# Four raw and three split weight slots, and modulation sums on an earlier, tighter schedule, in a two-block transformer kernel

## The reference, cut to what matters

```python
def hybrid_layer(x, c, positions, w_mod, b_mod, g_pre, g_post, w_in, w_out, ...):
    mod = jax.nn.silu(c) @ w_mod + b_mod          # 2048 x 6144 a layer
    shift, scale, gate = jnp.split(mod, 3, axis=-1)
    h = rms_norm(x, g_pre) * (1.0 + scale[:, None, :]) + shift[:, None, :]
    proj = h @ w_in
    ...
    out = y @ w_out
    return x + gate[:, None, :] * rms_norm(out, g_post)
```

## Time and profile before

| | |
|---|---|
| three runs | 3748.43, 3752.31, 3753.46 us; median 3752.31 |
| profiled execution | 3751.18 us, span 3749.5 us, mean granted TensorE clock 0.981 |
| TensorE busy | 3533.7 us, 94% |
| VectorE, ScalarE, GpSimd busy | 1865.1, 1322.7, 1155.9 us |
| DMA | 494.65 MB, mean 132 GB/s |
| chain that ended last | TensorE 66%, DMA 13%, VectorE 12%, ScalarE 6% |

### The profile page before, as it was taken

The page is one execution under the profiler, slowest core; times in us unless marked ns, Lnnn a source line. Parts: engine busy times, 40 slices in busy tenths (PEclk is TensorE's granted clock), DMA queues, the critical chain, the costliest instruction groups (busy, mean ns, idle before and its releaser), DMA issues.

```text
span 3749.5 us, 47967 instructions
## 1 busy us (share of the span) xinstructions
PE 3533.7 (94%) x17180; PEld 2823.6 (75%) x17180; DVE 1865.1 (50%) x3156; ACT 1322.7 (35%) x2206; POOL 1155.9 (31%) x1244
## 2 busy tenths in 40 slices
PE   6799999999879999999998999999998999999997
PEld 5667878887666678788876778877886778877885
DVE  4643376553565233765435535545535534645535
ACT  4212323332442223233325525423235525423223
POOL 5554766664362546666610000002000000002000
PEclk9999999999989999999999999999999999999999
DMA  8544454455674445544645632322345632322345
GB/s 274 150 105 123 130 137 129 119 152 176 193 233 116 113 126 133 139 121 125 194 126 157 183 91 61 94 68 62 121 150 174 181 91 62 93 68 65 121 147 173
DMA packets 232257, 494.65 MB, mean 132 GB/s; under 512 B 36030, under 2 KB 45177, under 8 KB 225896
## 3 DMA queue, kind: packets, MB, share of 16 engines
q1 hardware_dynamic: 181224, 356.57, 31.4%
q0 software_dynamic: 33536, 109.10, 11.0%
q10 hardware_dynamic: 17280, 26.07, 2.1%
HBM read 470.58 MB, written 24.75 MB: 132 GB/s over the span
## 4 chain that ended last, share of the span: by engine, by line
PE 66%; DMA 13%; DVE 12%; ACT 6%; issue 3%; DVEq 0%; SPq 0%; ACTq 0%; POOL 0%; POOLq 0%
PE bank L754 15%; PE bank L756 14%; PE bank L755 14%; DMA stage<-in_w_in 7%; DMA stage<-in_w_out 6%; DVE wlo L1693 5%; PE bank L882 4%; ACT whi L1223 3%; PE bank L902 3%; PE bank L868 2%; PE bank L749 2%; PE bank L751 2%; PE bank L750 2%; PE bank L891 2%; PE bank L1006 1%
## 5 line engine op out<-in xcount | busy, mean ns | idle before, releaser
L754 PE MATMUL bank<-wlo,act_hi 128*128 128x512 f32 (+1 forms) x3712 | 1524.3, 411 | 153.4 <-DVE wlo L1693 135.7
L756 PE MATMUL bank<-whi,act_lo 128*128 128x512 f32 (+1 forms) x3712 | 1457.2, 393 | 0.0
L755 PE MATMUL bank<-whi,act_hi 128*128 128x512 f32 (+1 forms) x3712 | 1455.8, 392 | 0.0
L1693 DVE TENSOR_TENSOR wlo<-stage,whi 128x1024 fp32r<-128x1024 f32 (+1 forms) x624 | 825.5, 1325 | 870.8 <-ACT whi L1223 867.8
L754 PEld LDWEIGHTS bank<-wlo,act_hi 128*128 128x128 f32 x3712 | 709.6, 191 | 370.7 <-DVE wlo L1693 166.8
L1223 ACT ACTIVATE whi<-stage 128x1024 fp32r<-128x1024 f32 (+1 forms) x624 | 646.5, 1040 | 956.3 <-DMA stage<-in_w_in 455.7
L756 PEld LDWEIGHTS bank<-whi,act_lo 128*128 128x128 f32 x3712 | 709.0, 191 | 151.9
L755 PEld LDWEIGHTS bank<-whi,act_hi 128*128 128x128 f32 x3712 | 711.4, 192 | 137.1 <-issue 7.7
L2642 POOL TENSOR_TENSOR macc<-macc,mprod 128x512 f32<-128x512 f32 x360 | 509.5, 1415 | 66.5 <-POOL mprod L2635 66.5
L2635 POOL TENSOR_SCALAR mprod<-wmod,csil 128x512 f32<-128x512 f32 x384 | 314.8, 820 | 427.1 <-DMA wmod<-in_w_mod 243.7
L2680 POOL DMA_DIRECT2D macc<-in_gla_w_gate_up x4 | 2.1, 528 | 1117.0 <-DVE Y L2291 1117.0
(11 more groups left out here) (259 smaller groups left out, 3223.9 us busy)
## 6 DMA issues: line engine op xcount, KB each, us to landing
stage<-in_w_in SPq DMA_DIRECT2D x400, 512.0 KB, 3.7
wmod<-in_w_mod POOLq DMA_DIRECT2D x384, 256.0 KB, 3.2
stage<-in_w_out SPq DMA_DIRECT2D x192, 512.0 KB, 3.8
out<-Y ACTq DMA_DIRECT2D x20, 1024.0 KB, 6.3
zone<-out SPq DMA_DIRECT2D x8, 2048.0 KB, 12.2
stage<-in_w_in SPq DMA_DIRECT2D x32, 320.0 KB, 3.6
Y<-in_x SPq DMA_DIRECT2D x4, 1024.0 KB, 7.4
rpb_tiles<-rpb_pad POOLq DMA_DIRECT2D x16, 224.0 KB, 5.6
```

Source lines behind the costliest of these rows:

```text
L754: pe.matmul(out, hi_x, lo_w, start=(k == 0), stop=False)
L755: pe.matmul(out, hi_x, hi_w, start=False, stop=False)
L756: mm = pe.matmul(out, lo_x, hi_w, start=False, stop=(k == KC - 1))
L1693: dve.tensor_tensor(wlo[:, j % RH, :, 0:width], stage[:, j % RS, :, 0:width], whi[:, j % RH, :, 0:width].bitcast(F32), ALU.subtract).then_ ...
```

## The change

Four things change. `RS`, `RH` become 4 and 3, and the slot of a pair goes by its number in the whole run (`cell`), so that three slots can go round. The column sums stand at written-out steps, `SUM_AT`, all within panels 2 to 11, and `unit_steps` keeps products off these steps. GpSimd begins a layer's modulation when bank 3 of the layer's first halved panel has been taken (`lin_free[3]`). The old activations are loaded tile by tile, each load behind two pairs of set 15, and `residual` waits for its own tile only. The first transposes of y move from row block 12 to 13 and wait for all twelve rows.

```diff
-RS, RH = 2, 4
+RS, RH = 4, 3
-MOD_AT = {2: 0, 3: 1, 4: 2, 5: 3, 6: 4, 7: 5, 8: 6, 9: 7, 10: 8, 11: 9, 13: 10, 14: 11}
+SUM_AT = {44: 0, 58: 1, 70: 2, 82: 3, 97: 4, 109: 5, 121: 6, 134: 7, 147: 8, 160: 9, 173: 10, 186: 11}
...
-    free = [s for s in range(first, first + 3 * n) if (s + UNIT_PV) % KC not in (ROW_SUM, ROW_SUM + 1)
+    free = [s for s in range(first, first + 3 * n) if s + UNIT_PV not in SUM_AT
...
+        def cell(blk, l, w, j):
+
+            return ((2 * NSET if blk else 0) + l * (NSET, NSET2)[blk] + w) * ND + j
...
-                sp.dma_start(stage[:, j % RS, :, 0:width], src.rearrange("o (a p) n -> p (o a) n", p=P))\
-                  .then_inc(w_landed[j % RS].sem, 16)
+                c = cell(blk, l, w, j) % RS
+                sp.dma_start(stage[:, c, :, 0:width], src.rearrange("o (a p) n -> p (o a) n", p=P))\
+                  .then_inc(w_landed[c], 16)
...
-                for h in range(2):
-                    first = (2 * h + 2 * to) % TT * DM
-                    sp.dma_start(view(first, 2, DM), x_dram[:, 2 * h:2 * h + 2, :]).then_inc(end_in.sem, 16)
-                out_set(blk, l, w + 1, NPS[blk] - 3)
+                for t in range(TT):
+                    out_set(blk, l, w + 1, NPS[blk] - 3, 2 * t, 2 * t + 2)
+                    sp.dma_start(xs(to, t), x_dram[:, t, :]).then_inc(end_in.sem, 16)
...
-                if blk == 0:
-                    at[4] = lambda: mod_row_sum(l, MOD_AT[NP - 2])
...
-                if k == ROW_SUM and p in MOD_AT:
+                if s in SUM_AT:
                     pe.wait_ge(fin_done.sem, fin_done.at(0, l, sum(a + UNIT_PV < s for a in UNIT_AT)))
-                    mod_row_sum(l, MOD_AT[p])
+                    mod_row_sum(l, SUM_AT[s])
...
-                            pe.wait_ge(mod_ev.sem, mod_ev.at(0, l, 10))
+                            pe.wait_ge(mod_ev.sem, mod_ev.at(0, l, NIN))
...
-                        at[12] = y_ahead
+                        at[13] = y_ahead
...
-                weights(0, l, NIN + 3, NIN + 1, at={4: lambda: mod_row_sum(l, MOD_AT[NIN + 1])})
+                weights(0, l, NIN + 3, NIN + 1)
...
-                dve.wait_ge(end_in.sem, end_in.at(blk, l, 32))
+                dve.wait_ge(end_in.sem, end_in.at(blk, l, 16 * (t + 1)))
...
-                pool.wait_ge(x_new.sem, x_new.at(0, l, -2))
+                pool.wait_ge(lin_free[3].sem, lin_free[3].at(0, l, 1))
```

More of the change, by code:

```diff
@@ L60 @@
 U_B, U_C, U_A = 0, 16, 32
-UNIT_TURN, UNIT_PV, ROW_SUM = 2, 4, 4
+UNIT_TURN, UNIT_PV = 2, 4
+SUM_AT = {44: 0, 58: 1, 70: 2, 82: 3, 97: 4, 109: 5, 121: 6, 134: 7, 147: 8, 160: 9, 173: 10, 186: 11}
 GATED_STEPS = (2, 3, 4, 5, 6, 7, 8, 9, 10, 12, 14)
 def unit_steps(first, n, gates=False):
-    free = [s for s in range(first, first + 3 * n) if (s + UNIT_PV) % KC not in (ROW_SUM, ROW_SUM + 1)
+    free = [s for s in range(first, first + 3 * n) if s + UNIT_PV not in SUM_AT
             and (s < GATE0[0] * KC or not gates or s % KC in GATED_STEPS)]
@@ L333, in build @@
         g_built = count("g_built", 16 * 2 * C_H)
-        w_landed = [count(f"w_landed{s}", 16 * NSET * ND // RS, 16 * NSET2 * ND // RS) for s in range(RS)]
+        w_landed = [sem(f"w_landed{s}") for s in range(RS)]
         hi_done = count("hi_done", NSET * ND, NSET2 * ND)
@@ L394, in build @@
         go_ev = count("go_ev", 0, TT)
-        end_in = count("end_in", 32)
+        end_in = count("end_in", 64)
         gain_in = count("gain_in", 16, 16 * 3)
@@ L735, in weights @@
                     pe.wait_ge(lo_done.sem, lo_done.at(blk, l, w * ND + j + 1))
+                    c = cell(blk, l, w, j) % RH
                     for a in range(2):
                         k = 2 * j + a
-                        hi_w, lo_w = whi[:, j % RH, a, 0:width], wlo[:, j % RH, a, 0:width]
+                        hi_w, lo_w = whi[:, c, a, 0:width], wlo[:, c, a, 0:width]
                         if n0 is not None:
@@ L820, in layer_end @@
                     at[2] = lambda: job0(*to, (KC + 6, 88)[to[0]])
-                if blk == 0:
-                    at[4] = lambda: mod_row_sum(l, MOD_AT[NP - 2])
                 weights(blk, l, n + 2, n - 1, HALF_BANKS[1][0], at=at)
-                if blk == 0:
-                    pe.wait_ge(mod_ev.sem, mod_ev.at(0, l, NIN))
                 if to:
@@ L908, in side1 @@
                 p, k = s // KC, s % KC
-                if k == ROW_SUM and p in MOD_AT:
+                if s in SUM_AT:
                     pe.wait_ge(fin_done.sem, fin_done.at(0, l, sum(a + UNIT_PV < s for a in UNIT_AT)))
-                    mod_row_sum(l, MOD_AT[p])
+                    mod_row_sum(l, SUM_AT[s])
                 if s - UNIT_PV in UNIT_AT:
-                    pv(l, UNIT_AT[s - UNIT_PV], sum(p_ * KC + ROW_SUM <= s for p_ in MOD_AT))
+                    pv(l, UNIT_AT[s - UNIT_PV], sum(a <= s for a in SUM_AT))
                 if s - UNIT_TURN in UNIT_AT:
@@ L1218, in split_hi @@
             def split_hi(blk, l, w, j, width=PW):
-                act.wait_ge(w_landed[j % RS].sem, w_landed[j % RS].at(blk, l, 16 * (w * (ND // RS) + j // RS + 1)))
+                c = cell(blk, l, w, j)
+                act.wait_ge(w_landed[c % RS], 16 * (c // RS + 1))
                 used, n = ring_free(blk, w, j)
                 act.wait_ge(used.sem, used.at(blk, l, n))
-                act.activation(whi[:, j % RH, :, 0:width], stage[:, j % RS, :, 0:width], ACT.Copy)\
+                act.activation(whi[:, c % RH, :, 0:width], stage[:, c % RS, :, 0:width], ACT.Copy)\
                    .then_inc(hi_done.sem, 1)
@@ L1407, in between @@
                         x_save(1, 2, (j - 5) // 2)
-                    if j == 6 and blk == 0:
-                        mod_row_out(l, MOD_AT[NP - 2])
                 return dict(between=between)
@@ L1486, in side1 @@
                 p, k = s // KC, s % KC
-                if k == ROW_SUM and p in MOD_AT:
-                    mod_row_out(l, MOD_AT[p])
+                if s in SUM_AT:
+                    mod_row_out(l, SUM_AT[s])
                 if s - UNIT_TURN in UNIT_AT:
@@ L1660, in _ @@
                 panel(0, l, NIN + 1, take_out_all(0))
-                mod_row_out(l, MOD_AT[NIN + 1])
                 layer_end(0, l)
@@ L1687, in split_lo @@
             def split_lo(blk, l, w, j, width=PW):
-                c = w * ND + j
-                dve.wait_ge(hi_done.sem, hi_done.at(blk, l, c + 1))
+                c = cell(blk, l, w, j)
+                dve.wait_ge(hi_done.sem, hi_done.at(blk, l, w * ND + j + 1))
                 used, n = ring_free(blk, w, j)
                 dve.wait_ge(used.sem, used.at(blk, l, n))
-                dve.tensor_tensor(wlo[:, j % RH, :, 0:width], stage[:, j % RS, :, 0:width],
-                                  whi[:, j % RH, :, 0:width].bitcast(F32), ALU.subtract).then_inc(lo_done.sem, 1)
+                dve.tensor_tensor(wlo[:, c % RH, :, 0:width], stage[:, c % RS, :, 0:width],
+                                  whi[:, c % RH, :, 0:width].bitcast(F32), ALU.subtract).then_inc(lo_done.sem, 1)
             def run(blk, l, w, width=PW, then=None, between=None, turned=None, ahead=None, take=None, side=None, s0=0):
```

## The result

The changed kernel takes 3779.06 us (median of 8 runs, 3770.48 to 3785.8) where the kernel before takes 3750.37 on the same chip: ratio 1.0072, 95% interval 1.0055 to 1.009. It is slower, as forecast, but by 29 us and not by 88. The profiled execution took 3776.36 us, its span 3774.7.

What follows compares the result with a forecast made beforehand. The prediction took GpSimd's modulation panels to bind the changed kernel, with TensorE waiting at the closer sums. 3749.5 + 127 (late at block 2) - 38 (block 2's raw slots) gave a 3838 us span, 3840 for the run; range 3760 to 3885.

Steps and rivals of the forecast that it cites:

- Rival 1: GpSimd's modulation panels hold TensorE at the moved sums: 3840 us, 3785 to 3885 with varied pace and halved sets; chance 0.70.
- 100 to 130: Sign of being right: TensorE waits some 100 to 130 us a layer for GpSimd's adds, in sums 5 to 11.
- 806 - 30 = 776: TensorE's arrival at layer 0's last sum, step 186: 806 us before, some 30 us sooner with the change.
- ten at 67.8: GpSimd's last ten modulation panels of a layer, each at the 67.8 us mean measured before the change.
- the 140.3 for the two panels before them: A layer's first panel at 62.7 us and second, with bias tiles, at 77.6, both measured in layer 1 before.
- rival 2: GpSimd quickens since VectorE, with which it competes, rests while TensorE waits: 64 us a panel, 3764 us; chance 0.12.
- border sets: Four halved sets before layer 1 take 97 us (123.3 before), four before block 2 take 101 (124.3 before).
- block 2: Without modulation there, four raw slots instead of two shorten its halved sets by 38 us together.
- GpSimd's start: Modulation begins after a layer's first two sets: 76 us in layer 0; 1147, 44 after layer begin, in layer 1.
- the case without cover: Three split slots instead of four slow block 1's full panels by 11 us if waits for GpSimd don't cover it.
- Rival 3: GpSimd is quick enough and the time falls, at 60 us a panel to 3684 us; chance of faster 0.07.
- Rival 4: Raw slots don't help, since VectorE's and ScalarE's own work sets the halved sets' pace: 3912 us; chance 0.09.

Runs made afterwards that it cites:

- experiment 2: Changed kernel with column sums and their accompanying steps at the old places; new slots, loads by tiles and GpSimd's later start kept: 3599.15 us, ratio 0.9587.
- experiment 6: Changed kernel without GpSimd's additions into the panel accumulator, products and signals kept: 3534.58 us, ratio 0.9431.
- experiment 4: Changed kernel with the old two raw and four split slots; moved sums, later start and loads by tiles kept: 3879.38 us, ratio 1.0346.
- Experiment 1: Kernel before with only the new slots (four raw, three split) and loads by tiles; sums and GpSimd's start as before: 3608.0 us, ratio 0.9625.
- experiment 8: New tiles, GpSimd's later start and old sum places, but two raw and three split slots instead of four and three: 3721.63 us, ratio 0.9924.
- experiment 5: Changed kernel with each panel's row of sums written as one 2 KB run instead of 512 elements of 4 bytes: 3654.18 us, ratio 0.9751.
- experiment 10: Changed kernel with each panel's first load issued during the last row block of the panel before: 3755.62 us, ratio 1.0017.
- 11: Changed kernel with both the row of sums written in one piece and each panel's first load issued ahead: 3615.77 us, ratio 0.9655.

## Why the prediction was right in its sign and wrong in its size

**Right: what binds.** Rival 1's mechanism is what happens. TensorE stands in front of sums 5 to 11 of each layer, 192 us in all, 97 and 95 us a layer where I gave 100 to 130. The spacing is shorter than GpSimd's panel, and no sum of the later half finds its panel done. Experiments 2 (sums back: 180 us less) and 6 (GpSimd's adds out: 244 us less) show it from two sides. TensorE's own way to the last sum was right too: its waits taken off, it comes to layer 0's at 871.9 - 96.9 = 775.0, where 806 - 30 = 776 was forecast. To the microsecond that is chance: with no waits at all, in experiment 6, it is there at 749.3.

**Wrong: the size of GpSimd's chain, 41 of 63 us.** The failed step is the price of that chain: the term "ten at 67.8" (measured 66.3 and 66.5) and the 140.3 for the two panels before them (135.4 and 132.5). I carried panels of before into the new order, and wrote of rival 2 that "the change takes none of it away". Next to it, 26 us too much stood in the border sets and block 2. The forecast of +88 is the difference of a large loss and a large gain, so 63 us of such errors, each 1 to 6 per cent of its term, leave a third of it.

```
us, layer 0 and layer 1                      forecast          measured            off
ten panels                                   678 + 678         663.0 + 664.7       -28.3
first and second panel                       140.3 + 140.3     135.4 + 132.5       -12.7
GpSimd's start (from 0, from layer 1's)      76 + 44           73.4 + 45.1          -1.5
last add to the halved sets                  112 + 112         114.4 + 114.1        +4.5
four halved sets at each border              97 + 101          91.8 + 94.4         -11.8
block 2                                      1660              1645.9              -14.1
```

(Block 2's forecast is 3838 - 2178. The column sums to -63.9, against 3774.7 - 3838 = -63.3 between the spans; the rest is rounding in the forecast.)

The pace is 66.3 to 66.5. Of the kernels with the later start and the scattered row write it is 68.0 where TensorE hardly waits for it (experiment 2; 67.9 in layer 1): the 67.8 was a good reading of that state, and fell by 1.7 when TensorE began to wait. (With the old slots, experiment 4, TensorE waits as well and it is 67.0 and 67.1.) By the table 1.0 of this is shorter waits for loads and 0.4 shorter adds; why the waits for loads shorten while TensorE stands, and why the first two panels came out shorter, no run shows. So rival 2, which lets panels fall to 64, was right that the pace moves and right in sign, but its reason is the smaller part: the adds were no more than 22.0 us against a floor of 15 x 1.26 + 0.61 = 19.5, and came to 21.6. That its time, 3764, lies only 15 us from the result is luck: at the measured pace its own arithmetic gives 3840 - 20 x 1.4 = 3812, and the first panels and the halved sets do the rest. In the same way the result, 3779, lies in the stated 3760 to 3885 only by the part that was added for rival 2; the binding case by itself was given 3785 to 3885.

**Wrong: the halved sets, 12 us at the borders and 14 in block 2.** I took 97 and named 91 as the bound. It is 91.8 (94.4 before block 2, where I took 101): the weights are ready for nearly every pair, and the granted clock is 1.00 where it was 0.90 before and 0.98 in experiment 4. Where the waits went, the slower clock went with them, so the lower bound was the value to take. Even a bound failed by this: for the run's first two sets I named 50.9 us, TensorE's busy time at a clock of 0.91, and they take 47.1 (23.6 to 70.7), busy 45.1 at 1.00. For layer 1's I had put it at full clock, 41 and took 44, and 42.3 were measured. In block 2 the halved sets give back 48 us where I had 38, and its full panels, left as they were in the forecast, 5 more (629.9 us twice, for 631.5 and 633.2).

**Right: split slots at no cost.** The changed kernel can't show it by itself, since the sums cover it, as the prediction says. Experiment 1 has no such cover. Its stretch of full panels, then that of the kernel before, layer 0:

```profile
121.70:883.90 762.20, 747.73 (x3598) 593.18 (x3598) 374.83 (x592) 227.97 (x377) 470.27 (x511) 1.00 0.49 137
154.20:915.90 761.70, 748.43 (x3597) 594.12 (x3598) 365.44 (x592) 228.10 (x378) 446.85 (x478) 1.00 0.48 133
```

In layer 1 it is 759.7 us for 767.4. The 11 us that I gave for the case without cover are not there. Where two raw slots stand, block 2 takes 3727.9 - 2022.1 = 1705.8 us with three split slots (experiment 8) and 1700.7 with four (experiment 4); that is one trace each, and experiment 8's is of an execution 8 us above its median, so it shows no cost either. No run has four raw and four split slots.

**Rival 3** (faster, at 60 us a panel) is what experiment 5 comes to. At its pace of 61.0 us the rival's arithmetic gives 3840 - 20 x 6.8 = 3704. Take from it the 36 us by which the rows of the table other than the first are off, and the 16 by which the first two panels are still shorter there (127.2 and 125.0 us), and 3652 is left; measured were 3654. Its condition, "half of the gap after a row write gone", was the right place to look. The change does not bring it; another edit does. **Rival 4**, that the raw slots don't help, is refuted by experiments 4 (100 us slower with two) and 8 (122 us slower with two than experiment 2).

What was argued only: that the profile's "issue" before the sums is GpSimd's add is by the agreement of times to 0.1 us and by experiment 6.

## What to carry to other kernels

An engine that runs free in a trace still has a pace, and moving its consumer to fixed, tighter places makes that pace the kernel's. Put the producer's time per item beside the consumer's spacing before moving anything. Then ask what the producer's item is made of: here a twelfth of it went with another engine's 2 KB write, and giving that write another shape took 125 us off without touching the engine that bound. When two parts of a change go opposite ways, run each alone: the slots gain 143 us, the moved sums lose 180. And where a change takes the waits out of a stretch whose granted clock is below 1.00, price the stretch at its matmuls' time at full clock: the border sets came out there.

## What the runs showed of the hardware that was not expected

- A 2 KB write of 512 elements of 4 bytes lands 8.4 to 11.4 us after its issue (all 24 of the changed kernel, median 9.8). GpSimd waits 7.0 us a panel for its 256 KB loads beside it, and 1.7 us beside the same 2 KB in one run.
- With the load issued earlier (experiment 10) the time in front of a panel's first product fell by 2.9 us in layer 0 and a third of it (1.0 us) came back at the products after it; with the row in one piece as well (11) nothing came back.
- Layer 0's full panels with GpSimd's adds gone: VectorE's split of a pair takes 1256 ns for 1460, and TensorE is busy 745.8 us for 752.9.
- Where TensorE waited more it also worked slower: seven waits of 97 us in all in layer 0's full panels stand beside a granted clock of 0.94, experiment 2's two of 14 us beside 0.98, and nearly the same matmuls kept it busy 765.7 us for 752.9. The 21 us of idle time that left the four sets before layer 1 took 31.5 us off them (123.3 to 91.8, clock 0.90 to 1.00).
